# A decoder layer on one core: staging of the retention stage, order of its transfers, late turned pieces, and part of the routing on GpSimd

## The reference

```python
n = rms_norm(h, norm1_g)
proj = n @ w_in                       # (1024, 1024) @ (1024, 6984): q_att, c_kv, q_idx, k_idx, w_idx, r_q, r_k, r_v, r_gate, g_att, g_ret
score = sum_h(relu(q_idx . k_idx) * w_idx)            # causal; the 256 best keys of a row
att = softmax(q . k * Dh**-0.5 - slope * dist) @ v    # over those keys, 8 heads, k and v shared
for each chunk of 128 rows:                           # retention, 4 heads, float32
    o = (q k^T * decay) v + (q * q_decay) state
    state = chunk_decay * state + (k * k_decay)^T v
y_ret = (silu(r_gate) * group_norm(o)) @ w_ret_branch
mixed = sigmoid(g_att) * (att @ w_att_branch) + sigmoid(g_ret) * y_ret
h = h + mixed @ w_out
h = h + hierarchical_moe(rms_norm(h))                 # best group of 4, best 2 of its 4 experts, SwiGLU
```

## Time and profile before

| what | us |
|---|---|
| median of 3 runs (lowest, highest) | 1558.13 (1553.03, 1560.5) |
| the profiled execution, its time | 1556.06 |
| its span in the trace | 1554.1 |
| PE busy | 1397.3 (90%) |
| DVE busy | 1111.5 (72%) |
| ACT busy | 872.6 (56%) |
| POOL busy | 670.5 (43%) |

### The profile page before, as it was taken

How to read it: one execution, slowest core, us unless ns; L and a number is a source line. 1 busy time by engine, 2 the same in 40 slices (tenths; PEclk the granted TensorE clock), 3 DMA queues, 4 the chain that set the end, 5 groups by cost and what they waited for, 6 DMA issues and landing times.

```text
span 1554.1 us, 19634 instructions
## 1 busy us (share of the span) xinstructions
PE 1397.3 (90%) x6518; PEld 1141.7 (73%) x6518; DVE 1111.5 (72%) x1590; ACT 872.6 (56%) x1528; POOL 670.5 (43%) x461
## 2 busy tenths in 40 slices
PE   6979999999998766577999899999999499999995
PEld 6867788878877655455776788888788378888884
DVE  6817999999999543364651536798952689999994
ACT  5227644345945545555663446545334478888884
POOL 4611344544455423223101445555433257766645
PEclk9987999999999878788999999999999699999998
DMA  5987878885855699987703736666255599889995
GB/s 200 359 210 143 210 243 284 219 279 170 283 173 179 202 332 262 238 271 172 150 15 109 243 103 215 230 210 212 69 192 197 205 328 265 250 236 362 278 300 69
DMA packets 153363, 336.74 MB, mean 217 GB/s; under 512 B 14896, under 2 KB 32688, under 8 KB 149040
## 3 DMA queue, kind: packets, MB, share of 16 engines
q1 hardware_dynamic: 111904, 227.49, 43.1%
q0 software_dynamic: 28496, 82.85, 25.1%
q10 hardware_dynamic: 12864, 25.17, 4.3%
HBM read 323.92 MB, written 125.83 MB: 289 GB/s over the span
## 4 chain that ended last, share of the span: by engine, by line
PE 54%; DVE 22%; DMA 13%; issue 3%; ACT 3%; POOL 2%; SPq 2%; DVEq 0%; ACTq 0%; POOLq 0%
PE ps L966 15%; PE ps L967 15%; PE ps L968 15%; DVE hits L2135 7%; PE ps L1287 3%; DVE n_lo L2025 3%; DMA w_raw<-in_w_in 3%; DMA n_dram<-first_out 2%; PE ps L1421 2%; PE ps L1277 2%; DMA sums_dram<-in_w_ret 1%; SPq L731 1%; DMA gate<-proj_dram 1%; DVE dist L2098 1%; DMA t_raw<-turned_dram 1%
## 5 line engine op out<-in xcount | busy, mean ns | idle before, releaser
L2625 POOL TENSOR_TENSOR w_lo<-w_raw,w_hi 128x512 fp32r<-128x512 f32 (+1 forms) x264 | 381.0, 1454 | 521.3 <-ACT w_hi L1493 520.6
L1493 ACT CAST w_hi<-w_raw 128x512 fp32r<-128x512 f32 (+1 forms) x264 | 161.7, 616 | 334.9 <-PE ps L968 254.2
L966 PE MATMUL ps<-n_hi,w_hi 128*128 128x512 f32 x624 | 247.9, 397 | 24.0 <-DVE first_out L2220 11.4
L967 PE MATMUL ps<-n_lo,w_hi 128*128 128x512 f32 x624 | 246.0, 394 | 0.0
L968 PE MATMUL ps<-n_hi,w_lo 128*128 128x512 f32 x624 | 245.6, 394 | 0.0
L2563 DVE TENSOR_TENSOR e_lo<-e_raw,e_hi 128x2048 fp32r<-128x2048 f32 x93 | 213.3, 2296 | 25.3 <-ACT e_hi L1931 24.9
L966 PE MATMUL ps<-w_hi,n_hi 128*128 128x512 f32 (+1 forms) x528 | 203.9, 386 | 11.6 <-DVE n_lo L2025 6.9
L968 PE MATMUL ps<-w_hi,n_lo 128*128 128x512 f32 (+1 forms) x528 | 201.9, 382 | 0.0
L967 PE MATMUL ps<-w_lo,n_hi 128*128 128x512 f32 (+1 forms) x528 | 201.5, 382 | 0.0
L1931 ACT CAST e_hi<-e_raw 128x2048 fp32r<-128x2048 f32 x93 | 177.6, 1913 | 37.0 <-DMA e_raw<-in_w_up 20.7
L2758 POOL DMA_INDIRECT out<-e_y,dest x62 | 144.1, 2324 | 96.8 <-DMA out<-e_y,dest 62.7
(11 more groups left out here) (283 smaller groups left out, 2665.6 us busy)
## 6 DMA issues: line engine op xcount, KB each, us to landing
w_raw<-sums_dram SPq DMA_DIRECT2D x128, 256.0 KB, 3.4
e_raw<-in_w_gate SPq DMA_DIRECT2D x64, 512.0 KB
e_raw<-in_w_up SPq DMA_DIRECT2D x64, 512.0 KB
e_raw<-in_w_down SPq DMA_DIRECT2D x32, 1024.0 KB
w_raw<-in_w_in SPq DMA_DIRECT2D x80, 256.0 KB, 3.8
sums_dram<-in_w_in POOLq DMA_DIRECT2D x20, 1024.0 KB, 14.8
t_raw<-turned_dram SPq DMA_DIRECT2D x68, 256.0 KB, 3.9
sums_dram<-in_w_in SPq DMA_DIRECT2D x16, 1024.0 KB, 10.6
```

What stands on the lines that cost most here:

```text
L966: mm(out, a[0], b[0], start=first, stop=False, skip_group_check=skip)
L967: mm(out, a[0], b[1], start=False, stop=False, skip_group_check=skip)
L1493: nc.scalar.copy(w_hi[c % NH][:, :width], split_from(c)[:, :width]).then_inc(hi_ready, 1)
L2625: G.tensor_tensor(w_lo[c % NH][:, :width], split_from(c)[:, :width], w_hi[c % NH][:, :width].bitcast(F32), ALU.subtract).then_inc(lo_ready, 1)
```

## The change

Buffers: rT_out has four buffers in place of three, first_out four in place of two, in places of the constants and of `w_up`; `junk2` moves into the retention region; a pair `t_late` is added. Each kind now has two semaphores, and the wait in front of a head's pieces is for all of the head before.

SP: sums group 2 is copied behind chunk 3 of the projections. load_head(1) waits for turned piece 63 and not 67, in front of the ga chunks. In the stage, loads of a head, the next four chunks and the next gate stand in front of a head's stores. The last four turned pieces (of 68) are loaded into t_late and split inside attention, at steps 26, 30, 50 and 54. The m6 chunks are loaded at tile 3 and cast at step 40.

ACT: out_turn stands behind out_stats. DVE: the rest of the search stands in front of phase 1 of head 1. POOL: scale_rows(0) is done one head earlier, adds of groups 4 and 5 one head later, groups 6 and 7 are copied at tile 4 and added from tile 6 on. Routing: owner and fresh are computed by POOL (`owners`), with subtractions and clamps in place of comparisons, and slot_weights comes earlier on PE and DVE.

```diff
-        rT_out = [r1t(f"rT_out{i}", [P, BANK], at) for i, at in enumerate((18688, 17152, 17664))]
-        first_out = [r1t("first_out0", [P, BANK], 18176), sb("first_out1", [P, BANK], at=cst_at + 4 * K_TRI)]
-        junk2 = sb("junk2", [P, DV], at=up_at)
+        rT_out = [r1t(f"rT_out{i}", [P, BANK], at) for i, at in enumerate((18688, 17152, 17664, 18176))]
+        first_out = [sb(f"first_out{i}", [P, BANK], at=at) for i, at in enumerate(
+            (up_at, cst_at + 4 * K_TRI, cst_at + 4 * K_REL, cst_at + 4 * (K_REL + BANK)))]
+        junk2 = r1t("junk2", [P, DV], 7168)
...
+        t_late = [sb(f"t_late{i}", [P, BANK], at=cst_at + 4 * (K_REL + i * BANK)) for i in range(2)]
...
@@ SP
-                if c == proj_at - 1:
-                    for n in range(8, 12):
-                        copy_quarter(n)
...
                 load_chunk(proj_at + c)
+                if c == 3:
+                    for n in range(8, 12):
+                        copy_quarter(n)
...
             load_rk(1)
+            sp.wait_ge(t_lo, 64)
+            load_head(1)
             for c in range(ga, ga + 4):
                 load_chunk(c)
-            for u in range(64, 68):
-                load_turned_n(u)
-            sp.wait_ge(t_lo, 68)
-            load_head(1)
             load_gate(0)
-            for c in range(ga + 4, ga + KT):
-                load_chunk(c)
...
-            for i in range(2):
-                load_head(i + 2)
-                load_rk(i + 2)
+            for i in range(3):
+                if i < 2:
+                    load_head(i + 2)
+                    load_rk(i + 2)
+                else:
+                    sp.wait_ge(proj_stored[0], 96)
+                    load_q(0)
+                for c in range(ga + 4 * i + 4, ga + 4 * i + 8):
+                    load_chunk(c)
+                load_gate(i + 1)
                 store_first(i)
-                load_gate(i + 1)
-                for c in range(gb + 4 * i, gb + 4 * i + 4):
-                    load_chunk(c)
-            sp.wait_ge(proj_stored[0], 96)
-            load_q(0)
-            store_first(2)
-            load_gate(3)
             load_q(1)
             store_first(3)
...
@@ ACT
-                    at, before = (4 * h + n) % 3, (4 * h + n) // 3
...
-                    if before:
-                        act.wait_ge(ret_stored[at], 16 * before)
+                    if h:
+                        act.wait_ge(ret_stored[n % 2], 32 * h)
...
                 if i in (1, 2):
                     out_phase2(i)
                     out_phase1(i + 1)
-                    out_turn(i - 1)
                 hi(c)
                 out_stats(i)
+                if i in (1, 2):
+                    out_turn(i - 1)
...
-                    if m == 3 * HA:
+                    if m == 5 * HA:
                         for c in range(m6, m6 + NH - 1):
                             hi(c)
+                    if m in LATE_AT:
+                        turned_n_hi(NPC + LATE_AT.index(m))
@@ DVE
-                    if i or f >= 2:
-                        dve.wait_ge(first_stored[f % 2], 16 * (2 * i + f // 2))
-                    else:
-                        dve.wait_ge(proj_last, 64)
+                    if i:
+                        dve.wait_ge(first_stored[f % 2], 32 * i)
...
                 pick(1.5)
+            pick(8)
             out_phase1(1)
+            pick(1e9)
             out_phase2(0)
-            pick(1e9)
             keep_first(0)
@@ POOL
-                if i == 3:
-                    scale_rows(0)
                 for x in range(1, 4 if i < 3 else 1):
                     lo(c + x)
                 if i == 0:
                     copy_sums((4, 5))
-                else:
-                    add_sums(i - 1, (4, 5))
+                if i == 2:
+                    scale_rows(0)
+                if i >= 2:
+                    add_sums(i - 2, (4, 5))
             scale_rows(1)
             for t in range(2, NT):
                 scale_rows(t)
-                if t == 3:
+                if t == 2:
+                    add_sums(2, (4, 5))
+                if t == 4:
                     copy_sums((6, 7))
-                    for c in range(m6, m6 + NH - 1):
-                        lo(c)
-                if t >= 5:
-                    add_sums(t - 5, (6, 7))
+                if t >= 6:
+                    add_sums(t - 6, (6, 7))
+            for c in range(m6, m6 + NH - 1):
+                lo(c)
+            add_sums(2, (6, 7))
...
+            def owners():
+                pool.wait_ge(ranked, 1)
+                own = small[:, 384:415]
+                past = pre[:].rearrange("p a n -> p (a n)")[:, 0:31 * NE].rearrange("p (i e) -> p i e", e=NE)
+                seq(G.tensor_tensor(small[:, 368:384], small[:, 352:368], small[:, 336:352], ALU.add))
+                seq(G.tensor_tensor(past, cst[:, K_TI + 1:K_TI + 32].unsqueeze(2).to_broadcast([P, 31, NE]),
+                                    small[:, 368:384].unsqueeze(1).to_broadcast([P, 31, NE]), ALU.subtract))
+                seq(G.tensor_scalar(past, past, 0.0, 1.0, ALU.max, ALU.min))
+                for n in (8, 4, 2):
+                    seq(G.tensor_tensor(past[:, :, 0:n], past[:, :, 0:n], past[:, :, n:2 * n], ALU.add))
+                seq(G.tensor_tensor(own.unsqueeze(2), past[:, :, 0:1], past[:, :, 1:2], ALU.add))
...
```

More of the change, by code:

```diff
@@ L388, in program @@
         rk_in, gate_in, silu_done = sem("rk_in"), sem("gate_in"), sem("silu_done")
-        state_done, ret_stored = sem("state_done"), [sem(f"ret_stored{i}") for i in range(3)]
+        state_done, ret_stored = sem("state_done"), [sem(f"ret_stored{i}") for i in range(2)]
         o_mu, o_var, o_rstd, o_done = sem("o_mu"), sem("o_var"), sem("o_rstd"), sem("o_done")
@@ L846, in _ @@
                     load_q(t + 3)
-                if t == 2:
+                if t == 1:
+                    for u in (64, 65):
+                        load_turned_n(u)
+                if t == 3:
                     sp.wait_ge(sums_added, SUMS_GATES)
@@ L850, in _ @@
                         load_chunk(c)
+                if t == 4:
+                    for u in (66, 67):
+                        load_turned_n(u)
                 if t == NT - 1:
@@ L887, in _ @@
                 if c == branch_at - 8:
-                    for i in range(3):
-                        sp.wait_ge(ret_stored[i], 16 * ((4 * HR + 2 - i) // 3))
+                    for i in range(2):
+                        sp.wait_ge(ret_stored[i], 32 * HR)
                     sp.wait_ge(sums_added, SUMS_BRANCH)
@@ L1459, in down @@
                 last.then_inc(ey_full, 1)
+            slot_weights()
             turn_rows(Step(0))
-            slot_weights()
             def work(i):
@@ L1693, in out_turn @@
                     j, half = divmod(n, 2)
[L1694 removed]
                     name = ("rT", h, j, half)
[L1696 to L1697 removed]
+                    if h:
+                        act.wait_ge(ret_stored[n % 2], 32 * h)
                     bk.wait_full(act, name)
[L1699 removed]
+                    bk.read(A(rT_out[n][:], bank(name), ACT.Identity, scale=gains[:, GRT + 2 * h + j:GRT + 2 * h + j + 1]), name)
                     bk.wait_read(act, name)
                     row = (2 * h + j) * P
[L1702 removed]
+                    act.dma_start(ret_dram[row:row + P, half * BANK:(half + 1) * BANK], rT_out[n][:]).then_inc(ret_stored[n % 2], 16)
             def out_qT(t, g):
@@ L1710, in _ @@
                     keep_product(c // 4 - 1)
-                turned_n_hi(c + 3)
+                if c + 3 < NPC:
+                    turned_n_hi(c + 3)
                 if c < NPC:
@@ L1761, in _ @@
                     if t == 0 and g == 0:
-                        for i in range(3):
-                            act.wait_ge(ret_stored[i], 16 * ((4 * HR + 2 - i) // 3))
-                        act.wait_ge(first_stored[0], 16 * 8)
+                        for i in range(2):
+                            act.wait_ge(ret_stored[i], 32 * HR)
                     if t >= 2 and g == 0:
@@ L2234, in out_qT @@
                 if (t, g) == (1, 1):
-                    dve.wait_ge(first_stored[0], 16 * 8)
-                    dve.wait_ge(ret_stored[0], 16 * 6)
+                    for i in range(2):
+                        dve.wait_ge(ret_stored[i], 32 * HR)
                 dve.wait_ge(kq_hi_done, 2 + 2 * t + g + 1)
@@ L2270, in _ @@
                     out_qT(*q_turned_at(m - 1))
+                if m - 2 in LATE_AT:
+                    turned_n_lo(NPC + LATE_AT.index(m - 2))
             def n_part(r, q, k):
@@ L2749, in _ @@
             rstd2(1)
+            def owners():
[9 more added lines that the diff above has]
+                seq(G.tensor_tensor(own.unsqueeze(2), past[:, :, 0:1], past[:, :, 1:2], ALU.add))
+                seq(G.tensor_scalar(fresh[:, 0:1], own[:, 0:1], 1.0, None, ALU.min))
```

(6 more changed lines are left out.)

43 lines of the change are left out of this document (20 added, 23 removed).

## The result

The changed kernel takes 1540.71 us (median of 8 runs, 1538.49 to 1555.17) beside 1558.31 (8 runs, 1553.03 to 1564.95) for the kernel before on the same chip: ratio 0.9896, 95% interval 0.9862 to 0.9931, 17.6 us faster. Forecast were 1512 and a range of 1492 to 1538. The gain is there, at little more than a third of its forecast 46.5 us, and the time lies above the forecast's range.

The account below looks back on a forecast made before the run. PE was taken as full in projections and experts, its idle time lying in waits elsewhere. The terms -9.5 - 23 - 13.5 + 1 - 1.5 = -46.5 us gave 1511.6 on the median, said as 1512, range 1492 to 1538.

Parts of the forecast that it names:

- Step 1: Before the projections: moving four copies of sums group 2 out of the index stage closes PE's 10.5 us gap; 9.5 us off.
- the rival with chance 0.08: Before the projections: POOL's accumulates come last and take the 9.5 us gain away; 1521 us, chance 0.08.
- Step 2, start: Retention stage, head 1: its loads go out 13 us earlier; 4.6 us of PE's 11.2 us gap are won.
- Step 2, middle: Retention stage: chunk ga+8 lands at 571 beside POOL's copies, where ACT had it at 575.50; 4.5 us won.
- Step 2, end: Retention stage from 571: waits for stores, gate and q rows go, last rT_out at about 631; whole stage 23 us off.
- no charge: Attention: accumulate waits in front of scale_rows(1) and (3) end at 630 and 645, rows needed at 632 and 654; no cost.
- Step 3: Attention: PE's 13.45 us wait for POOL and some 3 more go, 3 allowed at tile 5; 13.5 off, late splits +1.
- Step 4: Routing: owner list on POOL, done a us before token, and slot_weights under the gather; 1.5 us off.
- that of the DMA queues: Retention stage: queues take turns by packet, ga+8 may come at 578; 8 us won instead of 23, 1527 us, chance 0.20.
- step 3's: Attention, tile 5: a POOL stall of the old 13.5 us returns and cancels the gain there; 1525 us, chance 0.08.
- POOL's owner list, the rival of step 4: Routing: POOL finishes the owner list late, 5 us lost instead of 1.5 won; 1518 us, chance 0.08.
- The sum of all: Whole kernel: all losing rivals happen together; up to 1553 us, chance 0.03.

Follow-up runs that it names:

- e4: Changed kernel with POOL's accumulates of sums groups 1 and 2 spread between splits of early projection chunks; ratio 0.9927 to the kernel before.
- e1: Changed kernel with weight chunks ga+8 to ga+11 issued on SP in front of head 3's loads instead of behind; ratio 0.9903 to the kernel before.
- e2: Changed kernel with the eight copies of sums groups 4 and 5 issued in pairs during the projections; ratio 0.9804 to the kernel before.
- f1: Changed kernel with accumulates of groups 4 and 5 rescheduled: one behind head 1's splits, three behind head 2's, two behind head 3's; ratio 0.9870 to the kernel before.
- f2: Changed kernel with the eighth copy of groups 6 and 7 issued by SP instead of POOL; ratio 0.9903 to the kernel before.
- g1: Changed kernel with groups 4 and 5 copied singly in projections, accumulates rescheduled, groups 6 and 7 copied behind scale_rows(5), old routing; 1501.79 us, ratio 0.9651 to before.
- f3: Changed kernel with copies of groups 4 and 5 one by one in the projections, their accumulates from head 0 on; 1520.31 us, ratio 0.9781 to before.

## Why the prediction was wrong

- **Step 1 (forecast 9.5, measured some 4 to 7).** The gap closed as told, and the rival with chance 0.08 happened beside it. POOL's first accumulates went out at 78.8 beside the copies, and the next step could follow only at 104.9, where I had the chain start at 97. Its last accumulate went out at 176.7, for 177.7 before, and PE waited 11.8 us for POOL behind it. I did not carry the start of the chain to its end. e4 took the chain away and won nothing: most of the gap came back as PE's waits for POOL and DVE inside the projections. I had DVE's 297.15 of 305 busy us in the earlier trace rows and named only PE as the bound there; which of the two sets the end is not shown.
- **Step 2, start (forecast 4.6, measured 7.3).** Right and better: phase 1 of head 1 began at 500.49, 13.4 us earlier, 6.1 of them from in front.
- **Step 2, middle (forecast 4.5, measured 0).** Chunk ga+8 was cast at 569.52, 6.0 us earlier than in the earlier trace rows, all of them from in front. The step that failed is the landing at 571: on the clock of before it is 575.6. The copies took 38.6 us from the first issue to the last landing, where I had 35, and SP's loads crept beside them: SP stood 17.80 us in one issue. I had let the queue take its issues at once, but e1 shows that the stall is a sign of the traffic and not the cause: the chunk issued without it was late as well. e2 shows that the copies are nearly the whole of it, 20.8 us of the stage.
- **Step 2, end (forecast to bring the sum to 23; 9.9 came).** Against the forecast the stage is 4.6 us late at ga+8, still 4.4 at head 2's turn (598.27), and 13.5 at attention. The missing 9 are POOL's accumulate, 13.88 us in its issue, now in front of head 3's means and splits (in the kernel before it stalled 9.57 us, one head earlier). I priced the accumulates' move at their landing, "no charge", and not at their issue. f1 gave 9.5 back.
- **Step 3 (forecast 12.5 net, measured 3.1, and in the other traces of this attention nothing).** The forecast put q 5's rows behind a stall of the copies and allowed 3 us. The stall came, 27.18, and the gap was 6.89; but f2 shows that q 5's load would have been nearly as late without it. The wait for rT_out's stores was not on my list at all: the accumulates that I had let stand in front of scale_rows(1) for free slowed them. With both transfers moved attention took 11.3 us less than before (g1), near the forecast.
- **Step 4 (forecast 1.5 gained; no gain seen).** POOL's list took 9.0 us, not 6.5, and was still done at the token. The price that I left out is on DVE: 4.78 us became 6.37. The Trainium skill (SBUF — State Buffer, Who interferes with whom) states that DVE in a two-port mode and GpSimd exclude each other from a shared port pair; I cited it for POOL and left its price out. This case's longer DVE operations agree, with DVE as the one that waits. But two 128x512 operations with two SBUF inputs, between them and beside POOL's list, took 0.69 us with it and without it, where the Trainium skill, as the forecast cites it, lets such operations contend too; the measurement decides.

Of the rivals, that of the DMA queues (0.20) comes near the stage: 8 us gained for the measured 9.9, and ga+8 at 578 for 575.6. That is in part luck, since it did not have the accumulate's stall that made the end late. With it came step 1's rival and half of step 3's; POOL's owner list, the rival of step 4, was not late. The sum of all was given 0.03 as if they were independent. In the stage and in attention the cause is of one kind, POOL's bulk transfers beside loads and stores that something waits for, and a range that took in two losers at a time was too narrow. The four losing rivals also add up to 1556 and not to the 1553 that the forecast gives. In its direction (faster, 0.92) the forecast was right.

## What to carry to other kernels

When a bulk transfer and a chain of small loads share the DMA engines, price the buffers and the order both with and without the bulk: here the same change was worth 10 us of the stage beside the copies and 17 with them elsewhere, in single traces. Move the bulk first, in single pieces to where nothing waits for the DMA engines, and ask of each DMA that is moved what stands behind its issue, not only when it lands. Before closing a gap of the bounding engine, see how full the other engines are over the whole stage behind it: closing one gap of 10 us there was worth 4 to 7, and a second one nothing.

## What the runs showed of the hardware

- POOL's issue of a DMA stalled at two places of its sequence of copies and accumulates. The first is the 26th of them, the second accumulate of groups 4 and 5: 9.5 to 14.3 us in ten traces, with eight copies in front or with only one accumulate (e2, 14.09). The second is the 40th, the eighth copy of groups 6 and 7: 23.9 to 27.7 us in twelve. Eight copies of groups 4 and 5 went out in 5.1 us. In the changed kernel both stalls end 0.2 to 0.3 us after the landing of the DMA just in front (617.12 and 705.73). Where that one had landed before, there was none: at the 26th in f1, f3 and g1, at the 40th in f2. That the stall belongs to a position in the sequence fits all of this; no run stalled at another one, none was made to try it, and what sets it stays open.
- SP's issue of one 0.5 MB load took 17.80 us beside POOL's copies (10.9 to 19.1 in the traces of the changed order), 2.68 to 4.8 with the copies in the projections.
- A store of 256 KB landed after 2.9 us in the kernel before, and after 12.7 to 17.2 when it went out 1.4 to 2.4 us behind the first of two accumulates of 1 MB (nine traces).
- Two short DVE operations grew from 0.17 to 0.72 and 0.45 us, the same in nine traces, while POOL worked on SBUF beside them.
